# g_mix moved into the input weights, GpSimd scales the row tiles at the head, and the residual is read back from stored transposed rows

## The chip, the cores and the metric

The kernel runs on 1 core of one Trainium2 chip. The metric is the device time of one execution in microseconds, lower is better. The profile is one execution of the same program.

## The reference, cut to what matters

One decoder layer is computed for 1024 prompt rows and 8 sample rows (1032 rows in all) of width 2048, in fp32.

```python
def rms_norm(x, g):
    return x * lax.rsqrt(jnp.mean(x * x, axis=-1, keepdims=True) + EPS) * g

def mixer_inputs(x, g_mix, w_in):
    z = rms_norm(x, g_mix) @ w_in            # 2048 -> 6656 columns, 52 tiles of 128
    ...                                      # split into q, k, v and gates of mixers A and B

def mixer_output(x, oa, ob, ga, gb, p, w_out, g_ple, w_pg, w_ple):
    ya = oa * jax.nn.silu(ga)
    yb = ob * jax.nn.silu(gb)
    h = x + jnp.concatenate([ya, yb], axis=-1) @ w_out      # x here is the residual
    gate = jax.nn.sigmoid(rms_norm(h, g_ple) @ w_pg)
    return h + (p @ w_ple) * gate
```

A last rms_norm with g_final makes the output. Between mixer_inputs and mixer_output stand dilated window attention (mixer A, 8 head pairs) and banded attention (mixer B), for the prompt rows and for the sample rows against caches.

## The kernel before, in words

All large products have the activations transposed: `act_hi` and `act_lo` hold 16 slices (index k) of 128 features by 1032 rows. A value is split in two parts, a rounded one (hi) and the rest (lo), and so is each weight; `three()` issues three matmuls for one k and one third of the rows (344 of them): hi*hi (L1070), lo*hi (L1071), hi*lo (L1072). A "unit" is 16 values of k times three matmuls for one weight tile of 128 columns and one third of the rows; three units make a tile. The program has five stages.

1. **Head.** Nine row tiles (eight of 128 rows, one of 8) are loaded (`x_in`, two buffers), squared and summed on ScalarE (L1273), the inverse root is made in four small VectorE instructions (`inverse_root`), and VectorE makes `x_n = x * 1/rms * g_mix` (L1584). TensorE turns it in 16 transposes (`x_turn`, L825), ScalarE copies the result to `act_hi` (L1268) and VectorE subtracts to get `act_lo` (L1575). The first four row tiles are turned before the first matmul; `X_LATER` says before which position (16 * unit + k) the others are turned.
2. **z stage.** 52 tiles of `w_in`. The last two run as a pair, k outermost. Attention runs beside it: the function `events()` puts its steps at positions, and every engine walks through the same list. Results go to `z_scratch` in DRAM and are loaded again (`zq`, `zk`, `zv`).
3. **y stage.** The gated outputs are loaded into `act_hi`/`act_lo` over the input slices.
4. **h stage.** 16 tiles of `w_out`, 14 one after the other and the last 2 as a pair. For each, `residual` makes the transposed residual anew: SyncE loads 128 columns of x in 7 pieces (`load_x_cols`), TensorE turns them, three transposes for each third of the rows (L1124), ScalarE copies the third from PSUM to `h_row` (L1452), and at the tile's end VectorE adds the product (L1869, `add_residual`), then squares and sums (L1875, L1876, `add_squares`).
5. **Gate stage** and final norm.

Weights come in groups of 4 values of k (128 x 512 elements, 256 KB). SyncE loads a group into one of two `w_raw` buffers once the group two before is split (`w_split`); GpSimd rounds it to `w_hi` (L807) and subtracts to `w_lo` (L809), into a ring of five slots; a slot is free when the last third of rows has used it (`w_used`, `produced`). So in the z stage groups part 1, 2 and 3 of the next tile are made ready during the last unit of the present tile. Each engine is one queue in program order, and a waiting instruction holds back all behind it.

Of the kernel before, what the change touches and what calls it, by code (L numbers as in the profile page):

```python
# [6 lines left out]
F32 = mybir.dt.float32  # L7
# [39 lines left out]
X_FIRST = 4  # L47
X_LATER = {4: 4, 8: 5, 13: 6, 19: 7, 27: 8}
# [118 lines left out]
def events():  # L167
# [12 lines left out]
    for u in range(GATE0, ZPAIR):  # L180
        put(16 * u, "o_load", u)
    put(152, "a_load")
# [70 lines left out]
def build(nc, a, o):  # L253
# [12 lines left out]
    yt_dram = nc.dram_tensor("yt_scratch", [HPAIR, P, S], F32, kind="Internal").ap()  # L266
    h_dram = nc.dram_tensor("h_scratch", [KT, P, R], F32, kind="Internal").ap()
# [13 lines left out]
    with ctx:  # L281
# [10 lines left out]
        hi32 = act_hi[:].bitcast(F32)  # L292
        psum = ctx.enter_context(nc.psum_tensor("psum", [P, 8, 512], F32))

        def at(place, *tensors):
# [10 lines left out]
        x_in, x_n, g_row = at(W_END, ("x_in", [P, 2, D], F32), ("x_n", [P, 2, D], F32), ("g_row", [P, D], F32))  # L306
# [35 lines left out]
        h_stage, acc, h_row, sq, x_cols, ones, pt_hi, pt_lo, gcol = at(  # L342
            B0, ("h_stage", [P, 3, R], F32), ("acc", [P, R], F32), ("h_row", [P, 2, R], F32), ("sq", [P, T3], F32), ("x_cols", [P, 2, 9, P], F32),
            ("ones", [P, P], F32), ("pt_hi", [P, 2, R], F32R), ("pt_lo", [P, 2, R], F32R), ("gcol", [P, KT], F32))
# [71 lines left out]
        def _(sp):  # L416
# [16 lines left out]
            for i, (r0, n) in enumerate(ROW_TILES):  # L433
                if i >= 2:
                    sp.wait_ge(sem("x_normed"), i - 1)
                sp.dma_start(x_in[0:n, i % 2, :], x_p[r0:r0 + n, :] if i < 8 else x_s).then_inc(sem(f"x_loaded{i % 2}"), 16)
                if i == 0:
                    sp.dma_start(ident[:], a["c_ident"]).then_inc(sem("consts"), 16)
                    sp.wait_ge(sem("x_loaded0"), 16)
                    sp.dma_start(g_row[:], bcast_rows(a["g_mix"][0:1, :], P)).then_inc(sem("consts"), 16)  # L440
                elif i == 1:
                    sp.dma_start(pick[:], a["c_pick"]).then_inc(sem("consts"), 16)
                elif i == 6:
                    sp.wait_ge(sem("consts"), 48)
                    sp.dma_start(gcol[:], a["g_ple"].rearrange("a (k p) -> p (a k)", p=P), allow_slow_non_contiguous=True).then_inc(sem("consts"), 16)
                for g in {1: (0, 1), 2: (2,), 3: (3,), 5: (4,)}.get(i, ()):
                    weights(g)
# [1524 lines left out]
```

## Time and profile before

| | |
|---|---|
| median of 3 runs | 2419.85 us (2416.12 to 2421.75) |
| the profiled execution | 2420.02 us, its span 2418.2 us |
| TensorE matmul busy | 2350.7 us, 97% of the span |
| VectorE, ScalarE, GpSimd busy | 853.3, 669.6, 765.8 us |
| granted TensorE clock | 0.993 of full speed |

The span runs from the first to the last instruction that the profile records; 1.8 us of the execution lie around it. An engine that is busy for 97% leaves 67 us in which it does no matmul; where they lie is to be read from the waits.

### The profile page before, as it was taken

To read this page: it belongs to the slowest core of one execution; us is meant where nothing else is said; L and a number is where in the kernel's file an instruction comes from. 1 tells how busy PE (TensorE), PEld (TensorE's weight loads), DVE (VectorE), ACT (ScalarE), POOL (GpSimd) and SP (SyncE) were. 2 spreads that over 40 slices of the span, in tenths; PEclk is the share of its full clock that TensorE was granted. 3 is DMA by queue.
4 is the path that set the end of the run, shared out by engine and by line. 5 is a ranking of instruction groups with operands and counts; after the bars stand their busy time and mean duration, and the time that the engine had idled before them with its cause. 6 is when DMAs were issued, how large, how long until landed. Compare 5 with 4: busy or idle time off the path is not lost.

```text
span 2418.2 us, 40441 instructions
## 1 busy us (share of the span) xinstructions
PE 2350.7 (97%) x16009; PEld 2227.5 (92%) x16009; DVE 853.3 (35%) x2328; ACT 669.6 (28%) x1985; POOL 765.8 (32%) x783
## 2 busy tenths in 40 slices
PE   5999999999999999999999999999999999999997
PEld 4999999999999999888878899999999999999997
DVE  7013323323323404555555525242122362211243
ACT  5122222222222313334545411120000132221444
POOL 2322222222222222222122233333333334454564
PEclk9999999999999999999999999999999999999998
DMA  5233234233233224444444354543232354333685
GB/s 189 68 111 98 75 109 101 76 110 98 78 110 101 78 94 124 137 132 137 135 138 145 115 164 134 166 136 104 87 99 79 124 158 128 104 109 106 179 242 189
DMA packets 383796, 294.26 MB, mean 122 GB/s; under 512 B 53807, under 2 KB 347927, under 8 KB 382319
## 3 DMA queue, kind: packets, MB, share of 16 engines
q1 hardware_dynamic: 342261, 249.43, 35.4%
q10 hardware_dynamic: 41347, 42.25, 5.2%
q8 instruction: 127, 2.08, 0.4%
q14 instruction: 61, 0.50, 0.1%
HBM read 225.38 MB, written 66.22 MB: 121 GB/s over the span
## 4 chain that ended last, share of the span: by engine, by line
PE 83%; DMA 6%; DVE 5%; ACT 2%; SPq 1%; POOL 1%; issue 1%; DVEq 0%; ACTq 0%; POOLq 0%
PE psum L1070 24%; PE psum L1072 23%; PE psum L1071 23%; PE psum L853 3%; PE psum L875 2%; PE psum L886 2%; PE psum L930 1%; DMA s_ring<-in_cache_a_k 1%; PE psum L945 1%; PE psum L958 1%; DMA y_in<-yt_scratch 1%; DVE x_n L1584 1%; PE psum L912 1%; POOL w_lo L809 1%; DMA w_raw<-in_w_ple 1%
## 5 line engine op out<-in xcount | busy, mean ns | idle before, releaser
L1070 PE MATMUL psum<-act_hi,w_hi 128*128 128x344 f32 x4032 | 1315.9, 326 | 4.3 <-POOL w_lo L809 2.7
L1072 PE MATMUL psum<-act_hi,w_lo 128*128 128x344 f32 x4032 | 1288.7, 320 | 0.0
L1071 PE MATMUL psum<-act_lo,w_hi 128*128 128x344 f32 x4032 | 1287.5, 319 | 0.0
L1070 PEld LDWEIGHTS psum<-act_hi,w_hi 128*128 128x128 f32 x4032 | 759.9, 188 | 15.0 <-issue 8.5
L1071 PEld LDWEIGHTS psum<-act_lo,w_hi 128*128 128x128 f32 x4032 | 759.3, 188 | 0.2
L1072 PEld LDWEIGHTS psum<-act_hi,w_lo 128*128 128x128 f32 x4032 | 759.0, 188 | 0.0
L807 POOL CAST w_hi<-w_raw 128x512 fp32r<-128x512 f32 (+1 forms) x352 | 221.0, 628 | 1544.1 <-PE psum L1072 1361.7
L809 POOL TENSOR_TENSOR w_lo<-w_raw,w_hi 128x512 fp32r<-128x512 f32 (+1 forms) x390 | 504.8, 1295 | 65.9 <-ACT w_hi L1523 37.6
L1667 DVE COPY prob_t<-psum 128x512 f32<-128x512 f32 (+1 forms) x56 | 35.5, 634 | 451.9 <-PE psum L886 451.9
L1934 DVE TENSOR_TENSOR t_gate<-psum,acc 128x344 f32<-128x344 f32 x48 | 24.8, 516 | 262.0 <-PE psum L1072 262.0
L1869 DVE TENSOR_TENSOR h_row<-psum,h_row 128x344 f32<-128x344 f32 x48 | 22.9, 516 | 242.4 <-PE psum L1072 230.8
L1331 ACT ACTIVATE prob_t<-psum 128x512 f32<-128x512 f32 (+1 forms) x56 | 30.9, 552 | 233.8 <-PE psum L886 233.8
L1320 ACT ACTIVATE prob<-prob,near 128x256 f32<-128x256 f32 (+3 forms) x128 | 72.0, 564 | 77.6 <-DVE near L1652 77.6
L1292 ACT ACTIVATE stage<-psum 128x344 f32<-128x344 f32 (+1 forms) x108 | 48.4, 448 | 146.8 <-PE psum L1072 145.7
L1452 ACT ACTIVATE h_row<-psum 128x344 f32<-128x344 f32 x48 | 21.9, 457 | 234.0 <-PE psum L1124 200.5
L1532 ACT ACTIVATE t_gate<-t_gate 128x344 f32<-128x344 f32 x48 | 23.6, 491 | 213.1 <-DVE t_gate L1934 211.3
L1703 DVE CUSTOM_DVE_ANT_0 prob_b<-psum,bias_b 128x256 f32<-128x256 f32 (+1 forms) x128 | 46.8, 403 | 99.7 <-PE psum L930 96.8
L1363 ACT ACTIVATE probt_b<-psum 128x512 f32<-128x512 f32 (+1 forms) x64 | 36.6, 571 | 131.3 <-PE psum L958 130.8
L1793 DVE TENSOR_TENSOR stage<-stage,o_in 128x344 f32<-128x344 f32 (+1 forms) x42 | 26.6, 633 | 116.1 <-ACT stage L1299 104.4
L853 PE MATMUL psum<-zk,zq 64*128 64x128 f32 (+3 forms) x416 | 67.3, 443 | 0.0
L1639 DVE CUSTOM_DVE_ANT_0 prob<-psum,bias 128x256 f32<-128x256 f32 (+3 forms) x128 | 58.2, 500 | 19.4 <-PE psum L853 19.4
L1373 ACT ACTIVATE prob_b<-prob_b,mx 128x256 f32<-128x256 f32 (+1 forms) x128 | 61.4, 481 | 0.0
(211 smaller groups left out, 2047.6 us busy)
## 6 DMA issues: line engine op xcount, KB each, us to landing
w_raw<-in_w_in SPq DMA_DIRECT2D x208, 256.0 KB, 3.1
w_raw<-in_w_pg SPq DMA_DIRECT2D x94, 256.0 KB, 3.0
w_raw<-in_w_out SPq DMA_DIRECT2D x64, 256.0 KB, 2.7
z_scratch<-stage ACTq DMA_DIRECT2D x72, 172.0 KB, 1.9
h_scratch<-h_row ACTq DMA_DIRECT2D x16, 516.0 KB, 2.7
x_in<-in_x_prompt SPq DMA_DIRECT2D x8, 1024.0 KB, 5.2
zq<-z_scratch SPq DMA_DIRECT2D x32, 256.0 KB, 3.9
o_scratch<-ot SPq DMA_DIRECT2D x32, 256.0 KB, 3.2
```

The lines of the kernel that those rows point to most:

```text
L807: pool.tensor_copy(w_hi[:, slot, 0:n], raw(g, n)).then_inc(sem("w_rounded"), 1)
L809: pool.tensor_tensor(w_lo[:, slot, 0:n], raw(g, n), w_hi[:, slot, 0:n].bitcast(F32), ALU.subtract).then_inc(sem("w_split"), 1)
L853: mm = pe.matmul(psum[:, 2 + h, col:col + w], queries(half), keys(half), start=True, stop=True)
L875: mm = pe.matmul(psum[HD * h:HD * h + HD, 6, c0:c1:step], values[:, HD * h:HD * h + HD], prob_t[:, h, x * P:(x + 1) * P], start=(c in (1, ...
L886: mm = pe.transpose(psum[:, 4 + h, x * P:(x + 1) * P], prob_of(n, c)[:, h, x * P:(x + 1) * P], ident[:])
L1070: pe.matmul(psum[:, bank, 0:T3], hi_w, hi_a[:, k, rows], start=(k == 0), stop=False, skip_group_check=True)
L1071: pe.matmul(psum[:, bank, 0:T3], hi_w, lo_a[:, k, rows], start=False, stop=False, skip_group_check=True)
L1072: return pe.matmul(psum[:, bank, 0:T3], lo_w, hi_a[:, k, rows], start=False, stop=stop, skip_group_check=True)
L1292: act.activation(stage[:, slot, 0:w], psum[:, u % 2, 0:w], ACT.Copy).then_inc(sem("bank_free"), 1)
L1320: m = act.activation(piece, piece, ACT.Exp, bias=st[:, 2 + h:3 + h], accum_out=st[:, 4 + h:5 + h])
L1373: act.activation(pr, pr, ACT.Exp, bias=m[:, 4 + h:5 + h], accum_out=m[:, 6 + h:7 + h]).then_inc(sem("b_exped"), 1)
L1639: m = dve.tensor_tensor_reduce(pr[:, h, col:col + nk], psum[:, 2 + h, col:col + nk], bias[:, h, u0:u0 + nk], SCALE, -3e38, ALU.add, ALU.ma ...
```

## The change

In the head `x_n` is now x * 1/rms without g_mix. The gain is applied to the raw `w_in` group on GpSimd, in place, before it is split (`gain`, a two-input instruction with the 4 gains of each partition spread over 128 columns); GpSimd also scales row tiles 2 to 8 in the order of the head, in four pieces each (`x_norm`), and VectorE only the first two. `HEAD` puts the 8-row tile first. There are three `x_in` buffers, and the squares go to a buffer of their own. The rows of g_mix broadcast to all partitions are no longer loaded; ident and the 16 x 128 gains come over ScalarE's queue. ScalarE's root takes mean and epsilon itself. Before the first matmul five row tiles are turned.

Because `act_hi + act_lo` now is x/rms, its 16 slices are stored to DRAM during attention (`x_save`, 32 stores of 128 x 1032), and rms itself as one row. In the h stage SyncE loads both parts of a slice and VectorE makes (hi + lo) * rms in two instructions over 1032 columns (`residual` on VectorE); transposes, PSUM copies and the loads of columns are gone.

```diff
-X_FIRST = 4
-X_LATER = {4: 4, 8: 5, 13: 6, 19: 7, 27: 8}
+HEAD = [8, 0, 1, 2, 3, 4, 5, 6, 7]
+X_FIRST = 5
+X_LATER = {12: 5, 15: 6, 18: 7, 26: 8}
+X_NEEDED = (4, 7, 9)
+BY_VECTOR = 2
...
+    for k in range(KT):
+        put(16 * (11 + 3 * k) + 5, "x_save", k)
...
+            for j, i in enumerate(HEAD):
+                r0, n = ROW_TILES[i]
+                if j - 3 >= BY_VECTOR:
+                    sp.wait_ge(sem("x_normed"), 4 * (j - 2 - BY_VECTOR))
+                elif j >= 3:
+                    sp.wait_ge(sem("x_normed_first"), j - 2)
+                sp.dma_start(x_in[0:n, j % 3, :], x_p[r0:r0 + n, :] if i < 8 else x_s).then_inc(sem(f"rows_loaded{j % 3}"), 16)
+                for g in {1: (0,), 2: (1,), 4: (2,), 5: (3,), 7: (4,)}.get(j, ()):
+                    weights(g)
...
+                elif e[0] == "x_save":
+                    k = e[1]
+                    sp.wait_ge(sem("x_lo"), 4 * len(HEAD))
+                    sp.dma_start(xh_dram[k], hi32[:, k, :]).then_inc(sem("x_saved"), 16)
+                    sp.dma_start(xl_dram[k], lo32[:, k, :]).then_inc(sem("x_saved"), 16)
...
-            def load_x_cols(i):
+            def load_residual(i):
                 par = i % 2
                 if i >= 2:
-                    sp.wait_ge(sem("r_turned"), 3 * (i - 1))
...
+                    sp.wait_ge(sem(f"h_stored{par}"), 16 * (i // 2))
+                    sp.wait_ge(sem("h_summed"), 3 * (i - 1))
+                sp.dma_start(h_row[:, par], xh_dram[i]).then_inc(sem(f"xh_loaded{par}"), 16)
+                if i:
+                    sp.wait_ge(sem("r_ready"), i)
+                sp.dma_start(x_low[:], xl_dram[i]).then_inc(sem("xl_loaded"), 16)
...
+            def gain(g):
+                what, i, k, n = GROUPS[g]
+                if what != "in":
+                    return
...
+                gains = g_mix[:, k:k + n].rearrange("p (x a) -> p x a", a=1).to_broadcast([P, n, P])
+                pool.tensor_tensor(raw(g, n), raw(g, n), gains, ALU.mult).then_inc(sem("w_gained"), 1)
...
+            def x_norm(j):
+                i = HEAD[j]
+                n = ROW_TILES[i][1]
+                pool.wait_ge(sem("x_inverted"), j + 1)
+                pool.wait_ge(sem("x_turned"), 4 * (j - 1))
+                for q in range(4):
+                    cols = slice(512 * q, 512 * q + 512)
+                    pool.tensor_scalar(x_n[0:n, j % 2, cols], x_in[0:n, j % 3, cols], small[0:n, 18 + i:19 + i], None, ALU.mult).then_inc(sem("x_normed"), 1)
+
+            for g in range(4):
+                gain(g)
+                split(g)
+                x_norm(g + BY_VECTOR)
+            for j in range(4 + BY_VECTOR, len(HEAD)):
+                x_norm(j)
+            gain(4)
+            for g in range(4, len(GROUPS)):
+                split(g)
+                if g + 1 < len(GROUPS):
+                    gain(g + 1)
...
-                for x, (c0, n) in enumerate(PIECES[t]):
-                    mm = pe.transpose(psum[:, 4, c0:c0 + n], x_cols[0:n, i % 2, 3 * t + x, :], ident[0:n, 0:n])
...
+            def residual(i):
+                par = i % 2
+                dve.wait_ge(sem(f"xh_loaded{par}"), 16 * (i // 2 + 1))
+                dve.wait_ge(sem("xl_loaded"), 16 * (i + 1))
+                chain(dve.tensor_tensor(h_row[:, par, :], h_row[:, par, :], x_low[:], ALU.add))
+                dve.tensor_tensor(h_row[:, par, :], h_row[:, par, :], x_rms[:], ALU.mult).then_inc(sem("r_ready"), 1)
```

GpSimd's queue at its start. The name before the arrow is what is written; L807/L838 round a weight group, L809/L840 make its rest. Before:

```order
6 L807 CAST w_hi<-w_raw 128x512 [waits w_loaded0]
8 L809 TENSOR_TENSOR w_lo<-w_raw,w_hi 128x512 [waits w_rounded]
9 L807 CAST w_hi<-w_raw 128x512 [waits w_loaded1]
10 L809 TENSOR_TENSOR w_lo<-w_raw,w_hi 128x512 [waits w_rounded]
11 L807 CAST w_hi<-w_raw 128x512 [waits w_loaded0]
```

And of the change:

```order
7 L822 TENSOR_TENSOR w_raw<-w_raw,small 128x512 [waits w_loaded0,gain_loaded]
8 L838 CAST w_hi<-w_raw 128x512 [waits w_gained,w_loaded0]
9 L840 TENSOR_TENSOR w_lo<-w_raw,w_hi 128x512 [waits w_rounded]
10 L850 TENSOR_SCALAR x_n<-x_in,small 128x512 [waits x_turned,x_inverted]
11 L850 TENSOR_SCALAR x_n<-x_in,small 128x512 x3
12 L822 TENSOR_TENSOR w_raw<-w_raw,small 128x512 [waits w_loaded1]
```

A gain now stands ahead of each split of `w_in`, and a row tile of four pieces behind each of the first four.

SyncE's queue in the h stage, between two sets of weight groups. Before:

```order
534 L427 DMA w_raw<-in_w_out 128x4x128 [waits w_split] x4
535 L686 DMA x_cols<-in_x_prompt 128x2x128 [waits r_turned]
536 L687 DMA x_cols<-in_x_prompt 88x128
537 L686 DMA x_cols<-in_x_prompt 128x2x128
538 L687 DMA x_cols<-in_x_prompt 88x128
539 L688 DMA x_cols<-in_x_prompt 128x2x128
540 L689 DMA x_cols<-in_x_prompt 80x128
541 L690 DMA x_cols<-in_x_sample 8x128
542 L721 DMA p_nat<-in_p_prompt 128x256 [waits p_turned]
```

And of the change:

```order
568 L701 DMA x_low<-xl_scratch 128x1032 [waits r_ready]
569 L731 DMA p_nat<-in_p_prompt 128x256 [waits p_turned]
570 L437 DMA w_raw<-in_w_out 128x4x128 [waits w_split] x4
571 L698 DMA h_row<-xh_scratch 128x1032 [waits h_summed,h_stored0]
572 L701 DMA x_low<-xl_scratch 128x1032 [waits r_ready]
```

Seven small loads became two whole ones, and they stand behind the four weight groups instead of ahead of them.

## Rows read from the trace of the kernel before

**Rows 1.** The page: busy us, share of the span, instructions.
```profile
PE 2350.7 (97%) x16009; PEld 2227.5 (92%) x16009; DVE 853.3 (35%) x2328; ACT 669.6 (28%) x1985; POOL 765.8 (32%) x783
```

**Rows 2.** Whom TensorE waited for: us in total, times, longest.
```profile
PE psum L825 <- DVE x_n L1584: 29.3, 8, 16.8
PE psum L1070 <- POOL w_lo L809: 5.3, 4, 2.6
...
PE psum L1124 <- ACT h_row L1452: 0.6, 1, 0.6
```

**Rows 3.** Timeline of the head: start us, us, engine, instruction [idle before, releaser].
```profile
13.04 0.15 DVE L1581 TENSOR_SCALAR small<-small 128x1 f32<-128x1 f32 x1 [12.18 <-DMA pick<-in_c_pick]
...
35.65 0.65 PE L1070 MATMUL psum<-act_hi,w_hi 128*128 128x344 f32 x1
...
41.72 2.04 ACT L1268 ACTIVATE act_hi<-psum 128x512 fp32r<-128x512 f32 x4
...
42.69 2.35 DVE L1584 SCALAR_TENSOR_TENSOR x_n<-x_in,small,g_row 128x2048 f32<-128x2048 f32 x1
...
44.06 1.92 ACT L1273 ACTIVATE x_n<-x_in 128x2048 f32<-128x2048 f32 x1 [0.31 <-DMA x_in<-in_x_prompt]
...
48.60 2.35 DVE L1584 SCALAR_TENSOR_TENSOR x_n<-x_in,small,g_row 128x2048 f32<-128x2048 f32 x1
```

**Rows 4.** Timeline of ScalarE's copies of finished units 1 and 2.
```profile
66.97 0.46 ACT L1292 ACTIVATE stage<-psum 128x344 f32<-128x344 f32 x1 [0.92 <-PE psum L1072]
...
74.63 0.45 ACT L1292 ACTIVATE stage<-psum 128x336 f32<-128x336 f32 x1
```

**Rows 5.** Timeline of GpSimd beside VectorE in the head.
```profile
14.31 2.35 DVE L1584 SCALAR_TENSOR_TENSOR x_n<-x_in,small,g_row 128x2048 f32<-128x2048 f32 x1
14.53 3.26 POOL L809 TENSOR_TENSOR w_lo<-w_raw,w_hi 128x512 fp32r<-128x512 f32 x1
...
27.20 2.48 DVE L1575 TENSOR_TENSOR act_lo<-psum,act_hi 128x512 fp32r<-128x512 f32 x4
...
27.84 1.28 POOL L809 TENSOR_TENSOR w_lo<-w_raw,w_hi 128x512 fp32r<-128x512 f32 x1
```

**Rows 6.** Timeline of GpSimd, groups of the tile that starts at 97.3.
```profile
96.52 0.61 POOL L807 CAST w_hi<-w_raw 128x512 fp32r<-128x512 f32 x1 [1.04 <-DMA w_raw<-in_w_in]
97.21 1.30 POOL L809 TENSOR_TENSOR w_lo<-w_raw,w_hi 128x512 fp32r<-128x512 f32 x1
```

**Rows 7.** Timeline: GpSimd, then TensorE, around the latest weight group.
```profile
1447.82 0.61 POOL L807 CAST w_hi<-w_raw 128x512 fp32r<-128x512 f32 x1 [6.37 <-DMA w_raw<-in_w_in]
...
1449.82 0.43 PE L1070 MATMUL psum<-act_hi,w_hi 128*128 128x344 f32 x1 [1.45 <-POOL w_lo L809]
```

**Rows 8.** Timeline of TensorE in the h stage, across one `residual`.
```profile
1597.96 0.32 PE L1070 MATMUL psum<-act_hi,w_hi 128*128 128x344 f32 x1
...
1598.43 0.46 PE L1124 MATMUL psum<-ident,x_cols 128*128 128x128 f32 x3
...
1599.23 0.32 PE L1070 MATMUL psum<-act_hi,w_hi 128*128 128x344 f32 x1
```

**Rows 9.** Timeline of VectorE at an h tile's end, and of the first product after it.
```profile
1919.50 1.40 DVE L1869 TENSOR_TENSOR h_row<-psum,h_row 128x344 f32<-128x344 f32 x3 [17.85 <-PE psum L1072]
```

**Rows 10.** Groups by tile: 1032-column VectorE work, and loads.
```profile
L1890 DVE SCALAR_TENSOR_TENSOR act_lo<-h_stage,gcol,act_hi x14: 1294/1382/2325, 1931.2 to 1965.0; 128x1032 fp32r<-128x1032 f32 x14
```

**Rows 11.** DMA issues by line: KB each, median us to landing; then two timeline rows.
```profile
w_raw<-in_w_in SPq DMA_DIRECT2D x116, 256.0 KB, 3.0
...
x_in<-in_x_prompt SPq DMA_DIRECT2D x8, 1024.0 KB, 5.2
...
gcol<-in_g_ple SPq DMA_DIRECT2D x1, 8.0 KB, 6.6
...
376.44 0.33 SPq L459 DMA_DIRECT2D zk<-z_scratch  x1
...
399.06 0.60 PE L853 MATMUL psum<-zk,zq 64*128 64x128 f32 x2
```

More of the change, by code:

```diff
@@ L291, in build @@
         pick = keep("pick", [P, 8])
-        hi32 = act_hi[:].bitcast(F32)
+        hi32, lo32 = act_hi[:].bitcast(F32), act_lo[:].bitcast(F32)
+        g_mix = small[:, 32:48]
         psum = ctx.enter_context(nc.psum_tensor("psum", [P, 8, 512], F32))
@@ L449, in _ @@
                 weights(g)
+            sp.dma_start(pick[:], a["c_pick"]).then_inc(sem("consts"), 16)
+            sp.dma_start(gcol[:], a["g_ple"].rearrange("a (k p) -> p (a k)", p=P), allow_slow_non_contiguous=True).then_inc(sem("consts"), 16)
+            sp.wait_ge(sem("x_inverted"), len(HEAD))
+            sp.dma_start(rms_dram[0, 0:S].rearrange("(i p) -> p i", p=P), small[:, 9:17], allow_slow_non_contiguous=True).then_inc(sem("rms_stored"), 16)
+            sp.dma_start(rms_dram[0, S:R].rearrange("(p a) -> p a", a=1), small[0:NB, 17:18], allow_slow_non_contiguous=True).then_inc(sem("rms_stored"), 16)
             def load_zq(kind, n, half):
@@ L713, in _ @@
             for i in range(HPAIR):
-                load_x_cols(i + 1)
                 if i < len(ROW_TILES):
@@ L1147, in _ @@
                         continue
-                    if k % WG == WG - 1 and k < KT - 1:
-                        residual(i, k // WG)
                     if i == 0:
@@ L1174, in _ @@
                     group_wait("out", HPAIR + i, k)
-                    if i == 0 and k % 2 and 3 <= k < 15:
-                        residual(HPAIR + (k - 3) // 6, (k - 3) // 2 % 3)
                     for t in range(3):
@@ L1459, in _ @@
             for i in range(HPAIR):
-                for t in range(3):
-                    residual(i, t)
                 h_store(i)
@@ L1561, in chain, with inverse_root @@
                 dve.wait_ge(sem("dve_chain"), done[0])
-            def inverse_root(n, square, root, out):
+            def inverse_root(square, root, out):
                 chain(dve.reciprocal(out, root))
@@ L1567, in inverse_root @@
                 chain(dve.tensor_scalar(root, root, 0.5, None, ALU.mult))
-                chain(dve.reciprocal(out, root))
+                dve.reciprocal(out, root).then_inc(sem("x_inverted"), 1)
             def x_lo_parts(i):
-                r0, n = ROW_TILES[i]
+                r0, n = ROW_TILES[HEAD[i]]
                 for q in range(4):
```

174 lines of the change are left out of this document (83 added, 91 removed).

## The prediction

> **What bounds the kernel now.** I read the page's busy line first: TensorE is busy with matmuls for 2350.7 of 2418.2 us [rows 1], so about 67 us of the span can be won by starting or feeding it better, and all else only by giving it less to do. The table of waits says where those 67 us are. 29.3 of them stand before the transposes of the head, and 5.3 before products that wait for a weight group from GpSimd; the ones before the h stage's transposes are 0.6 [rows 2]. The head is therefore the one stage that something other than TensorE sets. Its timeline shows two things. VectorE's first real instruction starts at 13.04, having waited 12.18 us for the small table `pick`, which stands behind the second row tile and the broadcast gains in SyncE's queue. From there on a row tile goes through every 5.91 us (x_n starts at 42.69 and at 48.60), and this is VectorE's own work: x_n 2.35, act_lo 2.48, and about 1.1 for the mean and the inverse root [rows 3, 5]. ScalarE needs less for a row tile, 1.92 for the square and 2.04 for the copies, with the small reads and roots some 4.3 [rows 3]. The first product starts at 35.65, with four row tiles turned, and unit 1 ends at about 66.97, from where units run without a gap at 7.6 us each [rows 3, 4].
>
> In the z stage GpSimd works in bursts. A unit of 7.6 us has four quarters of 1.9, and each frees one slot. For the tile that begins at 97.3 its last group (part 3) is ready at 97.21 + 1.30 = 98.5, and it is needed after three quarters, at 97.3 + 5.6 = 102.9. That is a slack of 4.4 us, and the tiles of the early z stage (before attention) repeat it [rows 6]. Nowhere else than around 1449 did TensorE wait in the z stage for weights for over half a microsecond: there a load landed 6.37 us late and the product waited 1.45 [rows 7].
>
> **The sum.** It is made against the profiled execution, 2420.02 us (span 2418.2 and 1.8 around it), which is 0.2 above the median of the runs.
>
> *Transposes of the residual.* A unit is 16 steps of three products in 7.6 us, so a step takes 0.47 [rows 4]. From the first product of one step to that of the second after it would be 0.94; with three transposes between them it is 1599.23 - 1597.96 = 1.27 [rows 8]. One third of the rows costs 0.33. There are 48 (14 x 3 and 6 in the pair): 15.9 us. With them goes the wait of 0.6 on ScalarE's copy [rows 2]. Gain 16.5. This is work of the engine that is always busy, so nothing can hide it.
>
> *What replaces it* is two VectorE instructions of 1032 columns a tile. None like it is in the trace; the nearest is the three-operand one over 1032 columns at 1.38 median [rows 10], 0.52 x 3 = 1.6 by the 344-column work. I take 2.8 us a tile. VectorE idles 17.85 us before the end of an h tile [rows 9], so it costs nothing as long as the data are there. SyncE issues the loads behind four weight groups of which the last waits for the end of the previous tile. So they start some 2 us into the tile, land by 7 (half a row tile's bytes each, at 5.2 for a whole [rows 11]), and the residual is ready by 12 of 22.6. Only tile 0 is different: its residual comes about 9 us after its end. The banks are wanted again when tile 2 starts, 22.6 us after, so TensorE doesn't see it. In the last pair the work falls between act_lo instructions and may push them 2.8 us; they had caught up there. Cost 0, bound 3.
>
> *Head.* VectorE has no x_n for seven of nine tiles and no wait for `pick`. I follow one tile through the queues. The first whole row tile lands at 1.1 + 5.2 = 6.3 [rows 11]; square, root and inverse take 1.9 + 1.4, its scaling on VectorE at most 2.35, so it is at TensorE at 11.8. g_mix comes as 8 KB of 4-byte pieces on ScalarE's queue like gcol, which landed after 6.6 [rows 11], so the first gain starts at about 8. The second whole tile's root is there at about 14.6, after ScalarE's order of work. From here GpSimd sets the pace: scaling is new, and I price a 512-column piece at 0.68, like the rounding with its gap (0.61, next start 0.69 later in [rows 6]), so 2.7 a tile. A weight group is 1.28 for the gain and 1.98 for the split, 3.3. So tile 2 of the head's order is scaled at 17.5, and 3, 4 and 5 each 6.0 later: 23.5, 29.4, 35.3. TensorE turns the fifth tile by 30.0 and then starts its products, 5.6 earlier than now. 12 values of k later, with the first ones slower as now, it is 36.6; the next two turnings (2.0 each) bring the end of unit 0 to 42.5. Now ScalarE is the slowest: with 4.3 a tile, tile 6's copies and act_lo end at 44.2, where unit 1 must wait for them. Tiles 7 and 8 are scaled by 45.4 and 49.6, turned from 45.4 and at 51.2, and unit 2 starts at 56.0. Before it started at 66.97 [rows 4]. Gain 11.0.
>
> The bounds of that: if a scaling piece costs what GpSimd's two-input work does (1.28), a tile is 5.1, scaling ends at 19.9, 28.2, 36.5, 44.8, 49.9, 55.0, 60.1, the first product starts at 37 and unit 2 at 64.2, and the gain is 3. If it costs 0.61 and VectorE's two tiles take half, it is 13. A per-partition scalar is not a second tensor, so I stay near the rounding. The Trainium skill, "GPSIMD Engine Reference", Engine selection, says GpSimd is about half as fast as VectorE on two inputs and roughly at line rate on one; by it the price is that of the rounding and the sum is the same, and read as its plain advice (no elementwise work there) it would be the lower bound.
>
> *Gains in the z stage.* 208 groups get 1.28 us more, 266 us of GpSimd work under TensorE's cover. Part 1's gain is done while GpSimd waits for the slot. Those of parts 2 and 3 come into the burst, less the 1.04 that part 3 now waits for its load [rows 6]: 2 x 1.28 - 1.04 = 1.5 late, of a slack of 4.4. Hidden. Where a load is itself late the whole gain shows: around 1449 it adds 1.3 [rows 7], and by the same reckoning over all tiles (the end of the last w_lo against three quarters of the tile's first unit) one other tile, two before it, has a slack of only 0.5 and gives 0.8. Cost 2.
>
> *Stores of the slices.* 32 stores of half a row tile's size each, in pairs once a tile, stand in SyncE's queue ahead of loads for attention. A pair could hold them up by what a whole row tile takes over a weight group, 5.2 - 3.0 = 2.2 us, and to be careful 5 [rows 11]. The load of zk issued at 376.44 is first used at 399.06, 22.6 us later [rows 11]. Hidden; if that cover were gone it would be 16 x 2.2 = 35 us.
>
> Sum: 2420.0 - 16.5 - 11.0 + 2.0 = 2394.5, predicted 2395 us. A measurement of this kernel tells about 0.2% (5 us) from no change.
>
> **The rivals.**
>
> *Scaling at the two-input price.* For it: nothing in the trace shows such an instruction. Against: one tensor input. The gain of the head is 3, the time 2420 - 16.5 - 3 + 2 = 2402.5.
>
> *GpSimd locked out.* In the head a w_lo that started 0.2 us after x_n on VectorE took 3.26, and beside act_lo, of which one input is in PSUM, 1.28 [rows 5]. So a VectorE instruction with several inputs in SBUF stops GpSimd until its end. The Trainium skill, "SBUF - State Buffer", SBUF: two separate sides, says just this of the shared pair of ports, held for the whole instruction; by that rule, the trace agrees, and the two-input gains lock VectorE out as well. Attention's sample part has many such VectorE instructions. 208 gains at, say, one collision in six of 2 us, of which a part reaches TensorE where the slack is small, is 5 to 10 us: 2400 to 2405.
>
> *Slower.* Part 3 is late by 2d - 1.04 if a gain takes d. It passes 4.4 at d = 2.7; by the reckoning over all tiles some seven have about 4.4, nine about 6.5, the rest up to 16. At d = 4.5 the delay is 8.0, which costs 3.6 in seven tiles and 1.5 in some nine, 39 us in all, and 2420 - 16.5 - 3 + 39 = 2440. It decides from d of about 4.2. The longest row like it is 3.26 with a lock in it. It would need a slow read of the spread-out gains.
>
> *It doesn't do what it says.* The transposes are surely gone, so no change at all would need a new stall of some 25 us, such as the 35 of the stores: 2427 with all of it, about 2415 with half.
>
> **How the numbers follow.** The forecast with its small terms has 0.72 (2388 to 2400), the two-input price 0.10 (2402), the lock 0.09 (2400 to 2405), the stores' stall 0.05 (2410 to 2430), a slow gain 0.04 (2425 to 2440). From 2388 to 2405 the first three lie, more than 0.8 together; with their tails outside, 2388 to 2406 holds 8 in 10. Faster by over 0.2% (below 2415): the first three and part of the fourth, 0.93; the same 0.03; slower 0.04.
>
> **What would show it.** First product at about 30 and unit 2 at about 56; x_n on GpSimd at 0.61 to 0.7 a piece; h tiles without a gap every 22.6 us, 1.0 shorter than now; gains at 1.28; TensorE's waits on w_lo in the z stage at 3 to 5 us. Wrong would make it: pieces at 1.2 or more, w_lo or gain means above 2, waits on zq, zk or f_w, or products waiting at the start of an h tile for `h_bank_free`.

## The result and the profile after

The changed kernel takes 2452.01 us (median of 4 runs, 2444.82 to 2456.28), the kernel before beside it 2418.53. The ratio is 1.0135 (95% interval 1.0113 to 1.0157): 1.35% slower, where 1% faster was forecast. The profiled execution took 2444.82 us with a span of 2443.0, 24.8 more than before. It is the fastest of the four, 7.2 us below their median, so the trace explains 24.8 of the 33.5 us by which the medians differ; the other 8.7 are taken up where the forecast is compared, under the transposes.

The page after, its busy line, answers to [rows 1]:

```profile
PE 2349.1 (96%) x15865; PEld 2220.6 (91%) x15865; DVE 916.3 (38%) x2354; ACT 651.1 (27%) x1937; POOL 1028.3 (42%) x1019
```

TensorE has 144 instructions fewer (the 48 x 3 transposes) and yet is busy for only 1.6 us less. GpSimd is busy for 262 us more. The time went into idle stretches and into matmuls at the low clock. Whom TensorE waited for (us in total, times, longest), which answers to [rows 2]:

```profile
PE psum L881 <- POOL x_n L850: 18.1, 19, 3.5
PE psum L1128 <- POOL w_lo L840: 15.9, 5, 6.0
PE psum L986 <- DVE mx L1736: 10.5, 4, 3.3
PE psum L1128 <- ACT stage L1333: 8.2, 6, 1.6
```

Four stretches of the execution became longer, and one view sorts them. It gives busy time by stretch, and I cut the span at ScalarE's copies of finished units 1, 12, 90, 138 and 149: the head, the plain units, the first attention stage, the second (with the sample part), the last units, and the rest. First the kernel before, then the kernel after. Columns: stretch, its length, busy us of PE, PEld, DVE, ACT and POOL with counts, granted clock, DMA share, GB/s.

```profile
0.00:67.00 67.00, 37.45 (x242) 34.57 (x243) 48.14 (x91) 38.34 (x67) 13.81 (x14) 0.95 0.51 171
67.00:152.40 85.40, 85.40 (x546) 84.97 (x545) 1.95 (x17) 9.76 (x33) 30.07 (x32) 1.00 0.34 98
152.40:928.70 776.30, 776.30 (x5538) 724.54 (x5538) 235.15 (x911) 200.84 (x651) 196.07 (x208) 1.00 0.35 94
928.70:1452.10 523.40, 509.93 (x3594) 449.54 (x3593) 262.01 (x865) 213.90 (x577) 125.26 (x128) 0.99 0.45 137
...
1541.80:2418.20 876.40, 853.02 (x5496) 848.30 (x5496) 268.47 (x384) 197.78 (x643) 372.61 (x372) 0.99 0.44 135
```
```profile
0.00:70.90 70.90, 42.79 (x242) 36.26 (x243) 31.91 (x85) 40.71 (x66) 58.30 (x48) 0.83 0.43 143
70.90:163.80 92.90, 87.55 (x546) 86.84 (x546) 1.95 (x17) 9.77 (x32) 45.88 (x48) 0.96 0.36 101
163.80:950.30 786.50, 778.01 (x5538) 724.54 (x5538) 255.63 (x911) 200.68 (x650) 305.22 (x314) 1.00 0.41 113
950.30:1493.50 543.20, 515.12 (x3594) 454.06 (x3595) 286.93 (x867) 214.07 (x576) 192.37 (x192) 0.97 0.44 134
...
1583.30:2443.00 859.70, 836.70 (x5352) 833.23 (x5352) 305.36 (x416) 176.87 (x595) 383.24 (x378) 0.99 0.47 149
```

Row by row: the head is 3.9 longer, the plain units 7.5, the first attention stage 10.2, the second 19.8, the last units 0.1, and the rest is 16.7 shorter. That is the +24.8. The first four are taken one by one.

**The head.** The timeline of GpSimd shows what a row tile costs there:

```profile
14.81 6.19 POOL L850 TENSOR_SCALAR x_n<-x_in,small 128x512 f32<-128x512 f32 x4
20.97 1.05 POOL L822 TENSOR_TENSOR w_raw<-w_raw,small 128x512 f32<-128x512 f32 x1
...
24.09 6.20 POOL L850 TENSOR_SCALAR x_n<-x_in,small 128x512 f32<-128x512 f32 x4
...
42.66 24.67 POOL L850 TENSOR_SCALAR x_n<-x_in,small 128x512 f32<-128x512 f32 x16
```

Four scaling pieces take 6.16 us from start to start, 1.54 each; the rounding of as many elements takes 0.61, and even the two-input gain 1.05. A row tile and a weight group together take 24.09 - 14.81 = 9.3 us, where the forecast had 6.0 and the kernel before 5.9 [rows 3]. ScalarE's copies of units 1 and 2, which stand in [rows 4] for before, come at 70.91 and 78.58. GpSimd waits for no other engine from 14.81 to the end of the last scaling at 67.33; 3.6 us after that unit 1 is copied. From 18.6 to 42.5 us TensorE, which got little work, was also granted 0.50, its lower level of 1.2 GHz. That did not lengthen the head: GpSimd was busy for 23.25 of these 23.90 us, and TensorE waited for it. The two stretches at the lower level (POOL is the fifth busy time):

```profile
18.60:42.50 23.90, 12.97 (x48) 9.34 (x48) 9.61 (x22) 12.09 (x18) 23.25 (x19) 0.50 0.38 122
86.80:93.60 6.80, 4.18 (x15) 4.18 (x16) 0.00 (x0) 0.28 (x1) 5.45 (x7) 0.50 0.15 42
```

**The plain units.** The second row above is one stall, 5.35 us long, and the low clock around it. Timelines of SyncE's queue, GpSimd and TensorE:

```profile
71.53 0.43 SPq L455 DMA_DIRECT2D gcol<-in_g_ple  x1
72.00 2.28 SPq L457 DMA_DIRECT2D rms_scratch<-small  x1
...
75.24 0.38 SPq L437 DMA_DIRECT2D w_raw<-in_w_in  x1
...
86.22 1.04 POOL L822 TENSOR_TENSOR w_raw<-w_raw,small 128x512 f32<-128x512 f32 x1 [7.87 <-DMA w_raw<-in_w_in]
...
89.42 0.65 PE L1128 MATMUL psum<-act_hi,w_hi 128*128 128x344 f32 x1 [5.35 <-POOL w_lo L840]
```

A weight load issued at 75.24 is there at about 86.2, 11 us later; such loads take 3.1 in the median. In the queue ahead of it stand transfers in 4-byte pieces: 8 KB of gcol, which landed after 3.8 us, and the two new stores of the roots, 4 KB in all. Since gcol had landed by 75.33, the stores are the likelier cause; the tenth run bears on it. SyncE came to them so late because a weight load in front waited for GpSimd; in the first experiment below they go out between 38 and 46 us, and the next weight load is issued only at 62.55.

**The first attention stage.** VectorE's work in it grew from 235.15 to 255.63 us though its instructions are the same 911. Its timeline, and GpSimd's beside it:

```profile
270.18 0.69 DVE L1700 COPY prob_t<-psum 128x512 f32<-128x512 f32 x1 [8.96 <-PE psum L942]
270.79 1.07 DVE L1643 TENSOR_TENSOR near<-near,n_stat 128x2 f32<-128x2 f32 x1
...
272.36 1.40 DVE L1650 TENSOR_SCALAR prob<-prob,near 128x256 f32<-128x256 f32 x2
...
278.34 0.17 DVE L1685 TENSOR_SCALAR near<-near 128x2 f32<-128x2 f32 x1
```
```profile
270.55 1.29 POOL L840 TENSOR_TENSOR w_lo<-w_raw,w_hi 128x512 fp32r<-128x512 f32 x1
272.47 1.14 POOL L822 TENSOR_TENSOR w_raw<-w_raw,small 128x512 f32<-128x512 f32 x1 [0.63 <-DMA w_raw<-in_w_in]
```

VectorE at the same place of the kernel before:

```profile
258.71 0.69 DVE L1667 COPY prob_t<-psum 128x512 f32<-128x512 f32 x1 [8.97 <-PE psum L886]
259.32 0.15 DVE L1610 TENSOR_TENSOR near<-near,n_stat 128x2 f32<-128x2 f32 x1
...
259.98 0.61 DVE L1617 TENSOR_SCALAR prob<-prob,near 128x256 f32<-128x256 f32 x2
...
264.36 0.17 DVE L1652 TENSOR_SCALAR near<-near 128x2 f32<-128x2 f32 x1
```

The instruction on two columns, 0.15 before, starts inside GpSimd's subtraction and ends with it (271.86 and 271.84); the pair of passes, 0.61 before, meets the gain. The subtraction is old work which now falls at another moment; the gain is new. From the block's first to its last instruction it is 8.16 us instead of 5.65. ScalarE waits for it with the copy of a finished unit behind, and TensorE waits for the bank. Timelines of ScalarE, then of TensorE:

```profile
278.54 0.48 ACT L1358 ACTIVATE near<-n_stat,near 128x1 f32<-128x1 f32 x2 [8.20 <-DVE near L1685]
...
280.66 0.44 ACT L1333 ACTIVATE stage<-psum 128x336 f32<-128x336 f32 x1
...
281.14 0.43 PE L1128 MATMUL psum<-act_hi,w_hi 128*128 128x344 f32 x1 [1.61 <-ACT stage L1333]
```

It comes back six times, which is the 8.2 us of the table of waits.

The cleanest pair of rows for the hold itself is where VectorE's instruction starts just behind GpSimd's. GpSimd and VectorE, of the change and then of the kernel before:

```profile
208.60 1.04 POOL L822 TENSOR_TENSOR w_raw<-w_raw,small 128x512 f32<-128x512 f32 x1
208.63 1.10 DVE L1685 TENSOR_SCALAR near<-near 128x2 f32<-128x2 f32 x2
```
```profile
197.13 0.60 POOL L807 CAST w_hi<-w_raw 128x512 fp32r<-128x512 f32 x1
197.17 0.66 DVE L1652 TENSOR_SCALAR near<-near 128x2 f32<-128x2 f32 x2
```

The first of the two VectorE instructions takes 1.03 us beside the gain and 0.59 beside the rounding, each time to the end of GpSimd's, and 0.17 alone. The same meeting, with the same times to 0.02 us, occurs seven times in this stage of either kernel. So GpSimd held VectorE before the change too, and the gain holds it for longer.

**The second attention stage.** The same 3594 matmuls are busy for 515.1 and not 509.9 us (lower clock), and TensorE is idle for 543.2 - 515.1 = 28.1 instead of 13.5 us. The largest single wait is 6.02 us for a weight group; the kernel before has its latest group near this place too [rows 7]:

```profile
1489.77 0.65 PE L1128 MATMUL psum<-act_hi,w_hi 128*128 128x344 f32 x1 [6.02 <-POOL w_lo L840]
```

### The profile page after: what moved, and what is told of

The parts are those of the page before. It is cut to its first block, busy times and chain, and to the rows that moved or that the text cites. A ratio compares the mean times of both kernels' runs of the same rounds, so it can differ in the third digit from the quotient of the medians.

```text
span 2443.0 us, 40326 instructions
## 1 busy us (share of the span) xinstructions
PE 2349.1 (96%) x15865; PEld 2220.6 (91%) x15865; DVE 916.3 (38%) x2354; ACT 651.1 (27%) x1937; POOL 1028.3 (42%) x1019
## 4 chain that ended last, share of the span: by engine, by line
PE 81%; DVE 5%; DMA 5%; POOL 4%; ACT 2%; issue 1%; SPq 1%; DVEq 0%; ACTq 0%; POOLq 0%
PE psum L1128 23%; PE psum L1130 22%; PE psum L1129 22%; PE psum L909 3%; PE psum L931 2%; PE psum L942 2%; POOL x_n L850 2%; DMA s_ring<-in_cache_a_k 1%; POOL w_lo L840 1%; PE psum L986 1%; PE psum L1014 1%; PE psum L1001 1%; DMA w_raw<-in_w_in 1%; DMA w_raw<-in_w_ple 1%; DMA w_raw_more<-in_w_ple 1%
## 5 line engine op out<-in xcount | busy, mean ns | idle before, releaser
L838 POOL CAST w_hi<-w_raw 128x512 fp32r<-128x512 f32 (+1 forms) x352 | 224.8, 638 | 1169.2 <-PE psum L1130 1109.4
L840 POOL TENSOR_TENSOR w_lo<-w_raw,w_hi 128x512 fp32r<-128x512 f32 (+1 forms) x390 | 503.7, 1293 | 64.5 <-ACT w_hi L1553 36.2
L822 POOL TENSOR_TENSOR w_raw<-w_raw,small 128x512 f32<-128x512 f32 x208 | 220.2, 1059 | 137.5 <-DMA w_raw<-in_w_in 125.3
L1980 DVE TENSOR_TENSOR t_gate<-psum,acc 128x344 f32<-128x344 f32 x48 | 24.8, 516 | 261.7 <-PE psum L1130 261.7
L909 PE MATMUL psum<-zk,zq 64*128 64x128 f32 (+3 forms) x416 | 67.3, 443 | 0.0
L1411 ACT ACTIVATE mx<-sink,mx 128x1 f32<-128x1 f32 x128 | 30.6, 286 | 131.1 <-DVE mx L1740 130.9
L1672 DVE CUSTOM_DVE_ANT_0 prob<-psum,bias 128x256 f32<-128x256 f32 (+3 forms) x128 | 58.2, 501 | 19.5 <-PE psum L909 19.5
```

The source lines that it names most:

```text
L822: pool.tensor_tensor(raw(g, n), raw(g, n), gains, ALU.mult).then_inc(sem("w_gained"), 1)
L838: pool.tensor_copy(w_hi[:, slot, 0:n], raw(g, n)).then_inc(sem("w_rounded"), 1)
L840: pool.tensor_tensor(w_lo[:, slot, 0:n], raw(g, n), w_hi[:, slot, 0:n].bitcast(F32), ALU.subtract).then_inc(sem("w_split"), 1)
L909: mm = pe.matmul(psum[:, 2 + h, col:col + w], queries(half), keys(half), start=True, stop=True)
L1672: m = dve.tensor_tensor_reduce(pr[:, h, col:col + nk], psum[:, 2 + h, col:col + nk], bias[:, h, u0:u0 + nk], SCALE, -3e38, ALU.add, ALU.ma ...
```

## The experiments

My account after this comparison, called theory A, was: GpSimd's scaling is dear, the gains lock VectorE out in attention and make weights late, the clock falls after stalls; the new residual and the stores are as forecast. Rival B blamed the 32 stores of the slices, rival C something else that comes with the new order. In all runs the change is taken against the kernel before timed beside it. In runs 2, 3 and 11 g_mix is missing from some or all of the product, so they serve to find the cause and are no version to use. The unit copies and stretches are single traces.

### 1. VectorE scales all rows, and 2. no gain on the weights

```
-BY_VECTOR = 2
+BY_VECTOR = 9          # and no x_norm on GpSimd
```


> Only edit: VectorE scales all nine row tiles, GpSimd none; the gains of g_mix on the weights stay. Theory A (a scaling piece on GpSimd costs 1.56 us and not 0.68, sixteen of them stand ahead of the weights of row tile 1, and the gains lock VectorE out during attention): the head gets back 14 us (unit 2's copy at about 64 to 68 us, not 78.6) and row tile 1 its 7 us, while the attention's loss stays; 2431 us, 2425 to 2438. Rival B (the loss after the head is the 32 stores of the slices on the DMA queues): the head's gain is the same, but the start of row tile 1 at 78.6 to 93.3 us stays 7 us longer than before; about 2438. Rival C (the scaling piece was slow only because VectorE held the port): VectorE's own scaling then keeps GpSimd's weight work out, and the head gains under 5 us; 2447.

```
 def gain(g):
-    if what != "in":
+    if what != "none":    # no gain on any group; split() doesn't wait for one
         return
```


> Only edit: the gain of GpSimd on the groups of w_in is left out (so g_mix is missing from the product); GpSimd still scales seven row tiles. Theory A (the gains lock VectorE out in attention, make weight groups late and let the clock fall): from row tile 1 on nearly all of the loss goes, 25 to 32 us; 2424 us, 2418 to 2430, with VectorE's 128x256 masking pass at 0.6 and not 1.4 us and ScalarE's copy of the unit in time. Rival B (stores of the slices): at most the two late groups come back, 2448. Rival C (the order of the new units or the clock alone): no more than 5 us, 2447.

The first takes 2432.2 us (ratio 1.0047, 1.0033 to 1.0062), 20 less than the changed kernel. Between the two traces the difference is 12.6 us: 12.3 are saved in the head (unit 1 copied at 58.56), 7.5 in the plain units, nothing in the attention stages (786.1 and 543.4), and 6.5 are lost behind unit 149, of which more below. The second takes 2409.71 (0.9967, 0.9951 to 0.9983), 42 less, and that is 14 below what I expected. By stretches of the profiled executions the gains' share is 4.5 us in the head (unit 1 copied at 66.41 and not 70.91), 3.3 in the plain units, and 10.2 and 19.5 in the attention stages; I had given them nothing in the head and too little after. Its scaling pieces (of the second run) are the clean measurement of that instruction. Their duration hardly varies, whatever VectorE does:

```profile
L848 POOL TENSOR_SCALAR x_n<-x_in,small x28: 1562/1566/1571, 13.8 to 61.3; 128x512 f32<-128x512 f32 x28
```

Columns: minimum, median, maximum in ns, first and last start, shapes. So 1.57 us is the price of the instruction, and rival C of the first run, that VectorE held it up, is out.

### 3. Both edits

> Both edits of the first two: VectorE scales all rows and no gain is made on the weights (g_mix is missing from the product); what is left of the change is the new order of the head, the stores of the slices and the residual from them. Theory A: the two parts add, and what is left is a gain of 16.5 us from the transposes and about 10 from the head: 2396 us, 2390 to 2402. Rival B (the stores cost 10 us or more): 2406 or more. Rival C (the new residual in the h stage costs what the transposes gave): 2410 or more.

2395.61 us (0.99, 0.9883 to 0.9917), as expected. Unit 1 is copied at 55.67. The busy time of the two attention stages:

```profile
141.10:917.40 776.30, 776.30 (x5538) 724.54 (x5538) 236.56 (x911) 201.00 (x651) 196.92 (x208) 1.00 0.41 115
917.40:1438.70 521.30, 508.09 (x3594) 448.43 (x3593) 259.64 (x865) 214.02 (x576) 125.88 (x128) 0.99 0.46 138
```

With GpSimd back to its old work the head gains 11.3 us, and both attention stages are as before (776.3; 521.3 against 523.4). What is left of the change is its gain.

### 4. The stores alone, on the kernel before

```
+for k in range(KT):
+    put(16 * (11 + 3 * k) + 5, "x_save", k)
...
+sp.dma_start(xh_dram[k], hi32[:, k, :])
+sp.dma_start(xl_dram[k], lo32[:, k, :])
```


> The kernel before with the 32 stores of the transposed slices added at the same places in the queue, and nothing else of the change (nothing reads them). Theory A (stores are hidden): within 2 us of before, 2418 to 2421. Rival B (the stores of 4.0 to 4.8 us each stand ahead of weights and V rows in the queue and starve TensorE): 2428 or more, up to 2440, with new waits on DMA loads between 78 and 700 us.

2419.23 us (1.0, 0.9988 to 1.0012). Rival B is out; units 12 to 90 take 776.3 us. These are the stores of the slices alone; the small stores of the roots are not in this run.

### 5. g_mix back in the rows

```
-dve.tensor_scalar(x_n, x_in, small[18 + i], None, ALU.mult)
+dve.scalar_tensor_tensor(x_n, x_in, small[18 + i], g_row, ALU.mult, ALU.mult)
...
+chain(dve.reciprocal(g_mix, g_mix))
...
-dve.tensor_tensor(h_row, h_row, x_rms, ALU.mult)
+dve.scalar_tensor_tensor(h_row, h_row, g_mix[:, i:i + 1], x_rms, ALU.mult, ALU.mult)
```


> The new order of the head, the stores and the residual from them stay; g_mix goes back into the rows (VectorE scales all nine row tiles by root and g_mix in one two-input pass, as before), no gain on the weights, and the residual is divided by g_mix with a column of reciprocals. Nothing is left out of the product. Theory A (with the gains and GpSimd's scaling gone nothing else of the change costs): what the run without gains gave, 2395.6 us, plus the second input of VectorE's nine passes, 2.35 instead of 1.29 us each as far as TensorE waits for them: 5 to 9.5 us; 2403 us, 2398 to 2407. Rival B (the head is then bound by ScalarE's squares, so the dearer pass is hidden): 2396. Rival C (fewer instructions and stores don't carry over once the product is whole): 2412 or more.

To make room for the rows of g_mix the squares, of which only the sum is used, go to a bf16 buffer here; ScalarE's square takes 1.9 us as before.

2402.39 us (0.9934, 0.9917 to 0.995), as expected. It leaves nothing out of the product, beats both kernels, and is the version to keep of those run here: 16 us better than before and 50 better than the change. VectorE's pass costs 2.35 us again, and unit 1 is copied at 65.47, 9.8 later than in the third run and only 1.5 earlier than in the kernel before. The dearer pass is not hidden (rival B's 2396 is out).

### 6. The gain as four one-input scalings

```
-pool.tensor_tensor(raw(g, n), raw(g, n), gains, ALU.mult)
+for q in range(n):
+    pool.tensor_scalar(raw(g, n)[:, q, :], raw(g, n)[:, q, :], g_mix[:, k + q:k + q + 1], None, ALU.mult)
```


> The first experiment (VectorE scales all rows, gains on the weights by GpSimd, 2432.2 us) with each gain made by four scalings of 128x128 by a column in place of one two-input product of 128x512; the arithmetic is the same. By the row-scaling piece (128x512, 1.57 us) four of them take 1.6 us or more against 1.07. Theory A1 (the loss in attention is the two-input gain keeping VectorE from its operands): VectorE's 128x256 masking passes are back at 0.6 us, the 10 us of the first attention stage come back, and the second stage, where weights are late, loses up to 10 more; 2424 us, 2418 to 2432. Rival A2 (any GpSimd instruction of that length does it, or it is GpSimd's time alone): first stage no better, second worse; 2440 or more.

2455.18 us (1.0153, 1.0134 to 1.0172), which is far over the total of A1 and yet splits the two mechanisms cleanly. Busy time by stretch, first of the first experiment, then of this one:

```profile
144.00:930.10 786.10, 777.84 (x5538) 724.39 (x5538) 263.24 (x911) 200.94 (x650) 305.56 (x313) 1.00 0.40 112
930.10:1473.50 543.40, 515.04 (x3594) 453.78 (x3595) 295.44 (x867) 214.24 (x577) 192.27 (x191) 0.98 0.44 134
```
```profile
143.10:919.40 776.30, 776.30 (x5538) 724.54 (x5537) 229.58 (x911) 200.89 (x650) 446.30 (x627) 1.00 0.42 113
919.40:1491.60 572.20, 522.89 (x3593) 460.33 (x3594) 261.27 (x867) 212.96 (x576) 282.75 (x385) 0.96 0.43 128
```

In the first attention stage GpSimd is busy for 446 instead of 306 us, and the stage is back at 776.3 us, to a tenth as before: it isn't GpSimd's time that hurts there but what its two-input instruction does to VectorE. I sorted VectorE's smallest instructions of that stage (128x2, one input) by what GpSimd was doing when they started. Beside nothing they took 0.17 us in the median; in this run beside a one-input scaling 0.24 (26 cases, at most 0.33). At the seven meetings shown above, which took 1.03 us beside the gain and 0.59 beside the rounding, they take 0.18 or 0.19 here. Those on two inputs took 0.96 beside the gain (10 cases in the changed kernel) and 0.16 beside the scaling (56 cases here, at most 0.31). In the second stage it is the other way round: VectorE is less busy (261 against 295 us), and TensorE's idle time in the stretch grows from 28.4 to 49.3 us. That stage pays for GpSimd's time: 126, 192 and 283 us of it in the third, first and this run give 521.3, 543.4 and 572.2 us, about a third of a microsecond for each. The line from the third run to this one, neither with the gain's hold on VectorE, gives 21.5 us for the first run's GpSimd time, of the 22.1 that it lost. That leaves little for the hold, but no run takes the hold alone out of this stage.

The Trainium skill, "SBUF - State Buffer", SBUF: two separate sides, lets VectorE instructions with two inputs in SBUF or in a two-port mode and GpSimd exclude each other from the shared ports for a whole instruction. The rows agree for GpSimd's two-input work (1.03 us beside the gain) and for its rounding (0.59). Beside its one-input scaling of 128x128, which takes 0.61 us, no 128x2 instruction took more than 0.33 us, so none was held for the whole of it.

### 7 to 9. Weight loads further back in SyncE's queue

In the second stage one wait has a visible path through the queue. SyncE in the first experiment, and at the same place of the kernel before:

```profile
1232.68 0.43 SPq L437 DMA_DIRECT2D w_raw<-in_w_in  x1
...
1233.78 0.43 SPq L604 DMA_DIRECT2D s_ring<-in_cache_a_v  x1
```
```profile
1224.46 0.43 SPq L427 DMA_DIRECT2D w_raw<-in_w_in  x1
...
1225.56 0.43 SPq L595 DMA_DIRECT2D s_ring<-in_cache_a_v  x1
```

The cache load goes out behind the weight load, and TensorE's wait for it ends at 1239.49 in the one and 1231.34 in the other, 5.7 and 5.8 us after the issue. So I moved the weight loads:

```
-put(16 * (3 * tile + 2) + 4 * (part + 1), "weights", g)
+put(16 * (3 * tile + 2) + 4 * (part + 1) + (8 if tile >= 28 else 0), "weights", g)
```


> The first experiment (VectorE scales, gains by GpSimd as one product, 2432.2 us) with the weight loads of row tiles 28 and later placed half a unit further back in the list that sets the order of SyncE's queue, so that cache and row loads of the second attention stage stand ahead of them; no engine's work is changed. Theory Q (in that stage a weight load waits in the queue for a raw slot that GpSimd frees later because of the gain, and the cache loads behind it come late): TensorE's waits for s_ring fall from 7.8 to under 5 us, those for mx from 10.1 to about 6, and less is lost at the low clock; units 90 to 138 take 534 us and not 543; 2422 us, 2416 to 2427. Rival P (GpSimd's pace alone makes the weights late, the queue doesn't matter): waits for w_lo grow instead, 2431 to 2440.

> The version with g_mix in the rows (2402.4 us) with the same later places of the weight loads. Theory Q: what is left of such waits there (mx 6.7, s_ring 3.9 us, 1.7 lost by the clock) falls by 3 to 6 us; 2398 us, 2394 to 2402. Rival P: weights late at unit bounds, 2402 to 2408.

> The kernel before with the same later places of the weight loads and nothing else. Theory Q: as in the version with g_mix in the rows, 3 to 7 us of 10.8 us of waits and 5.1 lost at the low clock come back; 2414 us, 2409 to 2418. Rival P: 2418 to 2424.

The results are 2429.12 (1.0042, 1.0027 to 1.0056), 2410.44 (0.997, 0.9958 to 0.9981) and 2426.18 us (1.0036, 1.0022 to 1.005): 3 less than the first experiment (its ratio was 1.0047, so hardly told apart), 8 more than the fifth, 8 more than before. The waits for s_ring fell as foretold, in the kernel with the gains from 7.8 to 4.5 us and in the kernel before from 4.5 to 2.8. But those for mx and w_lo grew: in the first by 1.3 and 1.8, in the second by 2.9 and 2.7. In the kernel before with this edit:

```profile
PE psum L930 <- DVE mx L1703: 8.0, 3, 4.3
PE psum L1070 <- POOL w_lo L809: 4.5, 2, 3.5
```

They were 5.1, 1.8 and 4.5. Theory Q holds for one wait and misses the stage: moving the loads moved the waits to others. By stretches, units 90 to 138 take 539.7 us instead of 543.4 in the seventh run, where 534 was expected; the stretch before takes 791.0 instead of 786.2, all of it ahead of unit 84, where no load was moved. In the ninth run these units take 526.3 instead of 523.4, and another 5.9 us are lost behind unit 149, again where no load was moved; why is open.

### 10. The small transfers first, and 11. gains in the first stage alone

```
+sp.dma_start(pick, ...); sp.dma_start(gcol, ...)
+sp.wait_ge(sem("x_inverted"), len(HEAD))
+sp.dma_start(rms_dram ...)                # both stores
 for g in range(5, 7):
     weights(g)
-...                                       # the same lines, from here
```


> The changed kernel with one edit in SyncE's queue: the small transfers of the head (pick, gcol in 4-byte pieces, the two stores of the root sums) are issued before weight groups 5 and 6 and not after them. Theory S (the 5.35 us that TensorE waits at 89.42 us, and the low clock around it, come from a weight load that lands 10.9 us after its issue behind these small transfers): unit 3 is copied 7.6 us after unit 2 and not 14.7; 2445 us, 2440 to 2450. Rival G (that group is late through GpSimd, whose last scaling pieces stand ahead of it): unit 3 stays 12 us or more after unit 2; 2450 to 2455.

2445.87 us (1.0113, 1.009 to 1.0135), 6 less than the changed kernel, in the middle of the expected range. Unit 3 follows unit 2 after 86.14 - 78.67 = 7.5 us, and the clock stays up:

```profile
78.70:93.70 15.00, 15.00 (x97) 15.00 (x96) 0.00 (x0) 0.89 (x4) 7.99 (x8) 1.00 0.27 82
```

So the 7.5 us of the plain units were a weight load behind small transfers, not GpSimd's work. A load behind the two stores of the roots is slow here too: issued at 60.46, it is there at 73.1, 12.6 us later, and gcol had landed long before. But at that time no product waits for it. The wait for x_inverted, now in front of two weight loads, cost nothing there.

```
-if what != "in":
+if what != "in" or i >= 30:
     return
```


> The second run's twin in between: VectorE scales all rows, and the gain of g_mix is made on the weights of row tiles 0 to 29 alone (so it is missing from the later tiles' product). If the two attention stages lose each by a cause of its own (the lock in the first, late weights and loads in the second): units 12 to 90 take 786 us as with all gains, units 90 to 138 take 521 as with none, and the head gives up 3 us; 2395.6 + 10 + 3 = 2408.5 us, 2405 to 2412. If the second stage's loss came from what the first leaves behind, or from the clock alone: 2415 or more.

2412.88 us (0.9971, 0.9958 to 0.9984), just over the expected range. Its second attention stage:

```profile
930.60:1456.70 526.10, 511.93 (x3594) 451.51 (x3593) 265.23 (x867) 214.30 (x577) 125.17 (x128) 0.98 0.46 137
```

The first stage, at 786.4 us, loses its 10 us, the second 4.8 against the third run (521.3) and not 22. So some 17 of the second stage's loss are its own gains'; the other 5 are within what this stage varies by from run to run (520.6 to 528.1 in the traces that have no gains in it).

## Why the prediction was wrong

| part | forecast | measured | shown by |
|---|---|---|---|
| transposes, new residual | -16.5 | -16.7 | stretch after unit 149 |
| head | -11.0 | +3.9 | runs 1, 2, 3 |
| plain units | 0 | +7.5 | run 10 |
| first attention stage | 0 | +10.2 | runs 3, 6 |
| second attention stage, last units | +2.0 | +19.9 | runs 3, 6, 11 |
| stores of the slices | 0 | 0 | run 4 |
| sum | -25.5 | +24.8 | |

*Transposes and residual: right in the mechanism; that 16.7 meets 16.5 is luck.* In the changed kernel's trace 16.7 came off behind unit 149. The two VectorE instructions of the new residual take 1.23 each, 2.5 a tile where 2.8 were taken. TensorE's busy time there fell by 16.3 us (853.0 to 836.7). In the runs 1, 3, 5 and 6 it fell by 13 to 15, and its idle time grew by 3 to 6, by single waits of mostly 1 to 3 us: for h_row, in the bound of 3, and for w_lo of the last stage. So the gain is real and a part of it can be lost again to what comes next. Of the ten traces with the new residual the changed kernel's has the shortest stretch there, 859.7 us; the others have 860.7 to 869.5 and the tenth run, which differs by the place of a few transfers in the head, 865.7. Against the one trace with 876.4 the usual gain is thus nearer 11 than 16.7, and this may be where most of the 8.7 us lie that the medians show and the trace does not; no trace of a slower execution shows it.

*Head: the step that failed is "scaling is new, and I price a 512-column piece at 0.68, like the rounding".* It takes 1.57, or 1.54 from start to start, outside of both bounds, since "what GpSimd's two-input work does" had been taken for the most a one-input instruction can cost. Unit 1 is copied at 70.9, where 56.0 was forecast and 64.2 was the bad end; the first product starts at 40.4 and not 30. The rest of the step was sound. Its own scheme, seven tiles from 14.8 on with three weight groups of 3.1 us between, ends the scaling at 67.3 when a tile is put at 6.17 us, and 67.33 was measured. The low clock has no part in it. The prediction's own sign of being wrong, pieces at 1.2 or more, came true. That the third run, where VectorE does the scaling, copies unit 1 at 55.7 and so meets the forecast's 56.0, is no check of this step, since GpSimd has no part of the scaling there. The rule set beside that step, that GpSimd is roughly at line rate on one input (the Trainium skill, "GPSIMD Engine Reference", Engine selection), does not hold for this instruction: 1.57 us against 0.61 for the rounding and 1.04 for a product with two inputs. Its plain advice, no elementwise work on GpSimd, does, since VectorE scales four times as many columns in 1.29 us.

*Plain units: not in the sum at all.* I had followed the DMAs of the head to their use, but not what a later head does to the small transfers behind them, nor what the new stores of the roots do to the weight load behind: it took 11 us to land, and TensorE stood for 5.35.

*Gains: the step that failed is "Hidden", with a slack of 4.4 us, and the 2 us.* The hiding failed in both attention stages. The slack was read from the early z stage alone, where it holds (with the small transfers out of the way no plain unit waits). In the second attention stage each microsecond more of GpSimd costs about a third of one (runs 3 and 6). And the rival "GpSimd locked out" had the right mechanism, even the sentence that "the two-input gains lock VectorE out as well", but a chance of 0.09 and a price of 5 to 10 us in the sample part. It cost 10.2 in the first attention stage, where I had seen no stall before and so looked for none: TensorE was busy there for 776.30 of 776.30 us, which looks like ample cover. It was not. Collisions on VectorE, 2.5 us of them in the block shown, make ScalarE's copy of a unit late and TensorE wait for some 1.5 us, at the same place of six pairs.

*Rivals.* The slower one asked for a gain of over 4.2 us a group; a gain takes 1.04. It ended on the right side by the wrong way. The forecast left 0.04 for slower because each mishap was priced by itself; four of them happened, and all four begin with the work given to one engine.

*Open.* Through which chain the waits for mx grow in the second stage (5.1 to 10.5 us) is not settled: runs 7 to 9 show that moving the loads shifts them, run 6 that GpSimd's time drives them. Whether the hold on VectorE adds to that stage's loss is argued above and not shown. I did not try the gain on another engine.

## What to carry to other kernels

Work that is moved to a lightly used engine must be priced by an instruction of its own form, and if the trace has none, the upper bound has to lie above the dearest neighbour. Before adding two-input work on GpSimd, look at VectorE's short instructions in every stage and at what waits behind them; a stage without one idle microsecond can still depend on them. A small store behind which a weight load stands belongs where nothing waits for that load. Of a bundle of edits, run the parts apart: here the parts that leave GpSimd alone gave 24 us, and those that use it cost 56.

## What the hardware did that I had not expected

- GpSimd's scaling of 128x512 by a column takes 1.57 us (1.562 to 1.571 in 28 cases), 2.6 times as dear as its rounding of the same size and half again as dear as its two-input product with a spread-out factor (1.04). On 128x128 it is 0.61.
- GpSimd's two-input gain holds up even a 128x2 instruction of VectorE until its end (1.03 instead of 0.17 us), and so does its rounding (0.59); the one-input scaling hardly does (0.24 in the median, 0.18 or 0.19 at the place of the 1.03).
- At stalls of 2 to 6 us, and while the head fed TensorE thinly, the granted clock went to 0.50, for 23.9 us in the head and 6.8 at the stall of the plain units. In the head this cost nothing, since TensorE was waiting for GpSimd.
- A 256 KB load took 10.9 us (changed kernel) and 12.6 us (tenth run) behind two stores that write 4 KB in 4-byte pieces, against 3.1 in the median. The 8 KB load in such pieces landed after 3.8 us.
